# Two-layer encoder on one core: odd heads' maxima moved, attention outputs read back early, four norms computed by token halves

## The reference, cut to what matters

```python
for l in range(2):
    sh1, sc1, g1, sh2, sc2, g2 = split(silu(c) @ ada_w[l] + ada_b[l], 6)   # 48 columns of 128 ("mods")
    if l == 1: k, v = shared_kv(modulate(x, kv_g, kv_shift, kv_scale))
    h = modulate(x, norm1_g[l], sh1, sc1)          # rmsnorm(x) * g * (1 + sc) + sh
    y = fox_attention(h) if l == 0 else sliding_window_attention(h, k, v)   # both end in @ w_o
    x = x + g1 * y
    h = modulate(x, norm2_g[l], sh2, sc2)
    u = h @ w_up;  u = conv3(u);  x = x + g2 * ((silu(gate) * val) @ w_down)
return rmsnorm(x) * final_g
```

## Time and profile before

| | |
|---|---|
| median of three runs | 2446.96 us (2446.95 to 2448.36) |
| profiled execution | 2450.65 us, of which the span of instructions is 2448.8 us |
| busy in the span | PE 2309.4, PE weight loads 1922.2, DVE 1535.8, ACT 1147.6, POOL 1173.5 us |
| granted TensorE clock, mean | 0.973 of 2.4 GHz |

### The profile page before, as it was taken

The page is one execution under the profiler, slowest core; times in us unless marked ns, Lnnn a source line. Parts: engine busy times, 40 slices in busy tenths (PEclk is TensorE's granted clock), DMA queues, the critical chain, the costliest instruction groups (busy, mean ns, idle before and its releaser), DMA issues.

```text
span 2448.8 us, 30449 instructions
## 1 busy us (share of the span) xinstructions
PE 2309.4 (94%) x10984; PEld 1922.2 (78%) x10984; DVE 1535.8 (63%) x2470; ACT 1147.6 (47%) x1934; POOL 1173.5 (48%) x1580
## 2 busy tenths in 40 slices
PE   5999999998989999999999899989899999999996
PEld 3778788886767888888888688878678888888884
DVE  6575656657677677777665686882564444545546
ACT  4475665748145333333333476771443333333334
POOL 5411313120546766666666352214366666666650
PEclk8999999999999999999999999989999999999998
DMA  7111211112831333333331313133111111111111
GB/s 266 53 48 35 69 35 55 42 56 78 309 112 42 117 121 121 121 125 123 124 119 59 127 34 77 53 110 122 35 43 52 52 52 57 56 52 52 52 52 69
DMA packets 66007, 206.91 MB, mean 84 GB/s; under 512 B 7345, under 2 KB 7985, under 8 KB 65730
## 3 DMA queue, kind: packets, MB, share of 16 engines
q1 hardware_dynamic: 29760, 109.06, 14.0%
q10 hardware_dynamic: 36098, 95.91, 12.0%
HBM read 186.66 MB, written 16.32 MB: 83 GB/s over the span
## 4 chain that ended last, share of the span: by engine, by line
PE 80%; DVE 9%; ACT 6%; DMA 3%; issue 2%; SPq 0%; POOL 0%; ACTq 0%; DVEq 0%
PE bank L917 50%; PE bank L632 19%; PE bank L792 1%; PE bank L766 1%; DVE H L1658 1%; PE bank L827 1%; PE bank L802 1%; PE bank L1088 1%; PE bank L828 1%; PE bank L829 1%; ACT PF L1226 1%; DMA ada_raw<-in_ada_t 1%; PE bank L648 1%; DVE tn L1653 1%; DVE ada_raw L1669 1%
## 5 line engine op out<-in xcount | busy, mean ns | idle before, releaser
L917 PE MATMUL bank<-H,w_spl 128*128 128x512 f32 x3744 | 872.3, 392 | 19.3 <-DVE H L1658 14.6
L917 PEld LDWEIGHTS bank<-H,w_spl 128*128 128x128 f32 x3744 | 708.0, 189 | 171.7 <-issue 16.2
L561 POOL TENSOR_TENSOR w_spl<-w_raw,w_spl 128x256 fp32r<-128x256 f32 x688 | 536.7, 808 | 426.7 <-ACT w_spl L1380 425.2
L632 PE MATMUL bank<-H,w_spl 128*128 128x512 f32 x2016 | 509.9, 401 | 19.1 <-DVE H L1658 11.6
L917 PE MATMUL bank<-TB,w_spl 128*128 128x512 f32 x2112 | 492.6, 389 | 0.0
L917 PEld LDWEIGHTS bank<-TB,w_spl 128*128 128x128 f32 x2112 | 396.1, 188 | 83.3 <-issue 0.8
L632 PEld LDWEIGHTS bank<-H,w_spl 128*128 128x128 f32 x2016 | 378.4, 193 | 98.1 <-issue 12.6
L1380 ACT ACTIVATE w_spl<-w_raw 128x512 fp32r<-128x512 f32 x328 | 196.8, 624 | 356.3 <-PE bank L917 300.5
L499 POOL TENSOR_TENSOR pace<-one_s 128x1 f32<-128x1 f32 x50 | 13.1, 262 | 682.9 <-PE bank L792 350.5
L1934 DVE SCALAR_TENSOR_TENSOR X<-bank,mods,X 128x1024 f32<-128x1024 f32 x176 | 225.2, 1280 | 45.5 <-PE bank L917 44.7
L1927 DVE TENSOR_TENSOR bank<-bank,sU 128x512 f32<-128x512 f32 x80 | 55.9, 699 | 302.6 <-PE bank L917 302.6
(11 more groups left out here) (172 smaller groups left out, 3180.1 us busy)
## 6 DMA issues: line engine op xcount, KB each, us to landing
w_raw<-in_w_stream SPq DMA_DIRECT2D x184, 512.0 KB, 3.7
ada_raw_f<-in_ada_t ACTq DMA_DIRECT2D x128, 256.0 KB, 2.9
ada_raw_o<-in_ada_t ACTq DMA_DIRECT2D x8, 2048.0 KB, 7.7
ada_raw<-in_ada_t SPq DMA_DIRECT2D x8, 1024.0 KB, 18.9
negF<-scratch_f ACTq DMA_DIRECT2D x16, 512.0 KB, 3.7
X<-in_x_t SPq DMA_DIRECT2D x4, 1024.0 KB, 10.9
X<-in_x_t ACTq DMA_DIRECT2D x4, 1024.0 KB, 8.3
scratch_x<-X ACTq DMA_DIRECT2D x1, 4096.0 KB, 12.7
```

The lines of the kernel that those rows point to most:

```text
L561: last = pool.tensor_tensor(block_at(layer, b, 1, q, q + 256), src[:, q:q + 256], block_at(layer, b, 0, q, q + 256).bitcast(F32), ALU.subt ...
L632: last = pe.matmul(dst, stat(k, a), mov(k, b), start=(k == 0 and a + b == 0), stop=(k == KT - 1 and a == 1))
L917: last = pe.matmul(dst, block_at(layer, b, x, k * P, k * P + P), mov(y), start=(start and x + y == 0), stop=(stop and x == 1), skip_group_ ...
```

## The change

1. **Maxima.** All heads use one row of `MAX_T` (it was another for the second head of a group), negation at task 8. So that the next q/k pair is there, `FILL_1` is 3 steps at four tasks and 2 at ten (it was 2 at sixteen).
2. **Head pairs early.** Pairs 0 to 5 are loaded at tasks 13 and 14 of the last group into Hf[:, k, 1] (the place of H's low part; ACT first waits for the last q/k step) and split at tasks 16 to 26; pair 6 at 34 and 41. O_rawA is gone.
3. **Output projection's first tile** of layer 0, k = 0 to 6, is issued at tasks 25 to 44 of the last group; k = 7 comes inside tile 1 (`out_two`).
4. **Mods.** For tiles 4 to 7 the g2 product leaves the output projection (three instead of four) and goes as 8 half products to pairs 2 and 3 of the FFN; the other 128 shift by one pair.
5. **Norms by halves.** The last two output tiles run half by half (6 and 7 of tokens 0 to 511, then 6 and 7 of 512 to 1023); the square sum and rstd of the first half are made while the second is multiplied, and the next stage (`first_pair`, K) starts with all k of half 0. So does the last down projection (`last_down`: all 8 tiles of half 0, then of half 1). Squares of the FFN's end are added by POOL. `t_sums` and the first `taps` change places, and `high(0, s)` of pair 2 comes after two copies.
6. **Shared K/V.** X * rstd is written into X itself, after SP has stored that half of X to DRAM, so `modulate(3)` needs no product of its own. The bias is loaded by SP, behind the second store.
7. **The end**: one DVE operation X * gain * rstd per half tile into Y (eight tiles of its own), 16 output DMAs of 256 KB on SP.

```diff
-MAX_T = [[2, 1, 1, 1, 1, 1, 1, 2, 2, 0, 0, 0], [0, 0, 2, 1, 2, 1, 2, 1, 2, 1, 0, 0]]
-MAX_T.append(MAX_T[0])
+MAX_T = [2, 1, 1, 1, 1, 1, 1, 2, 2, 0, 0, 0]
-FILL_1 = [2] * 16
+FILL_1 = [3] * 4 + [2] * 10
+HEADS_LOADS = {13: (0, 1, 2), 14: (3, 4, 5), 34: (6,)}
+HEADS_SPLITS = {16: 0, 18: 1, 20: 2, 22: 3, 24: 4, 26: 5, 41: 6}
+OUT_A_BESIDE = {25: (0,), 28: (1,), 31: (2,), 34: (3,), 37: (4,), 40: (5,), 44: (6,)}
...
+            def square_sum(n, h):
+                at_end = n == 4 and h == 1
+                pe.wait_ge(ss_done, SS_0[n] + (6 * h + 6 - at_end if n in (2, 4) else 6 + h))
+                pe.matmul(bank(h), ones[:], ss[:, half_of(h)], start=True, stop=False)
...
+                pe.matmul(bank(h), ones[:], sq_at(n, 7, h), start=False, stop=True).then_inc(sum_ps, 1)
...
+                    if g == NG - 1:
+                        out_first(0, OUT_A_BESIDE.get(T, ()))
...
+            def out_last(layer):
+                for h in range(2):
+                    for m in (LAST, LAST + 1):
+                        if h == 0:
+                            pe.wait_ge(w_ready, tile_order([W_OUT_A, W_OUT_B][layer] + m) + 1)
+                            pe.wait_ge(wo_ev, 10 * layer + m - 1)
+                        for k in range(KT):
+                            last = product(bank(4 + 2 * ((m + 1) % 2) + h), w_tile([W_OUT_A, W_OUT_B][layer] + m),
...
+                            if h == 1 and m == LAST and k == SUM_OUT:
+                                square_sum(1 + 2 * layer, 0)
...
+                    for h in range(2):
+                        for k in range(KT):
...
+                            pe.wait_ge(h_lo, H_0[[1, 4][layer]] + 8 * h + k + 1)
...
+                            if h == 0 and k == SUM_NEXT[1 + 2 * layer]:
+                                square_sum(1 + 2 * layer, 1)
...
+            for m in range(8):          # act: the squares of the last down tiles
+                down_square(0, m, 0)
+            for m in range(4):
+                down_square(0, m, 1)
+            root(2, 0)
...
+            tile(W_KV)                  # gpsimd
+            for m in range(1, 7):
+                add_squares(2, m, 0)
+            for m in range(1, 4):
+                add_squares(2, m, 1)
+            tile(W_KV + 1)
+            for m in range(4, 7):
+                add_squares(2, m, 1)
...
+                for m in range(LAST):   # vector: out_proj
                     if layer == 0:
                         mods_of_tile(m)
+                        if m == LAST - 1:
+                            mods_of_tile(LAST)
...
+                residual(LAST, 0)
+                add_squares(n, LAST - 1)
+                add_squares(n, LAST, 0)
+                residual(LAST + 1, 0)
+                half_scaled(hn, 0, 0)
+                half_scaled(hn, 1, 0)
+                residual(LAST, 1)
...
                 for kk in range(4):
+                    if kk == 2:
+                        taps(0, 0, pair(0))
+                        taps(0, 1, pair(2))
                     t_sums(kk)
...
-            for k in range(8):
-                scaled(5, k, y_done)
+            for h in range(2):
+                dve.wait_ge(rs_done, 1 + 2 * 3 + h + 1)
+                for k in range(KT):
+                    V_.scalar_tensor_tensor(Y[:, k, half_of(h)], X[:, k, half_of(h)], gain[:, G_FIN + k:G_FIN + k + 1],
+                                            rstd[:, half_of(h)], ALU.mult, ALU.mult).then_inc(y_done, 1)
```

More of the change, by code:

```diff
@@ L1347, in _ @@
             load_ada(1)
-            for m in range(7):
-                squares(1)(m)
+            for m in range(LAST - 1):
+                out_square(0, m)
                 load_ada(m + 2)
+            load_ada(7)
+            out_square(0, LAST - 1)
             def ffn(layer):
-                n0, d0 = BLOCKS * layer, 88 * layer
+                n0, d0 = BLOCKS * layer, 96 * layer
                 def t_high(kk, which):
@@ L1950, in ffn @@
                 for kk in range(4):
+                    if kk == 2:
+                        taps(0, 0, pair(0))
+                        taps(0, 1, pair(2))
                     t_sums(kk)
-                for p in range(NORMAL):
-                    taps(p, 0, pair(4 * p))
-                    taps(p, 1, pair(4 * p + 2))
-                    gated(p)
+                gated(0)
+                taps(1, 0, pair(4))
+                taps(1, 1, pair(6))
+                gated(1)
                 for p in range(NORMAL, PAIRS):
-                    with_ada = layer == 0 and p in ADA_PAIRS
@@ L2018, in _ @@
                 last.then_inc(kb_lo, 1)
-            modulate(3)
+            for k in range(KT):
+                low(3, k)
             for b in range(4):
```

668 lines of the change are left out of this document (428 added, 240 removed).

## The result

The changed kernel takes 2423.14 us (median of four runs, 2421.15 to 2426.74) beside 2447.66 us of the kernel before on the same chip: 0.990 of it, 95% interval 0.9883 to 0.9917, so 1% faster. The forecast was 2384 us, range 2371 to 2404. The direction was right; of the 63 us that were summed up, 29.7 came between the two profiled executions, and 24.5 between the medians.

The account below looks back on a forecast made before the run. PE was busy 2309.4 of 2448.8 us, so only its idle holes and half-clock time could be won. Gains 5 + 0 + 9 + 11 + 25 + 13 = 63 us off 2450.65, median 3.7 lower: 2384 us, range 2371 to 2404.

Parts of the forecast that it names:

- attention: All head groups, with moved maxima, fill and splits: about 5 us gained, bounds 0 and 10.
- output norms: Norm by halves between output projection and FFN: gain 9 us in layer 0 (bounds 5, 13), 11 in layer 1 (8, 15).
- four land in head 13 ... so it does not shrink (24 us): Last attention group: four of six forward-moved splits fall in head 13, DVE load about 22 us, head stays at 24.
- 0.8 us a group: Attention: gain from spreading the maxima over tasks 0 to 8, 0.9 us in the first group.
- Tile 0 beside the group: Layer 0 output tile 0 beside the last heads: gain 0, bound 10 us, since tile 2 waits for loads.
- output tile 0 pays: Rival: PE, not the loads, sets tile 2's start, 10 us more gained, 2374 us; chance 0.07.
- a new stall of 6.3 us: First Strassen pair of layer 1's FFN: PE waits for ACT's first product copy, 52.7 to 59.0 us behind tile 7.
- Norm behind FFN 0, K/V, queries, bias: From FFN 0's last down projection to the sliding window's scores: 25 us gained, bounds 19 and 27.
- K's half 0 ends at 36.6: K of the shared K/V: its first half ends 36.6 us behind the start of the last down projection.
- End: From FFN 1's last down projection to the kernel's end: 37.5 us against 50.9, gain 13, bounds 10 and 15.
- The second: Rival: helpers on DVE, ACT and POOL bind the halves in four norms, costing up to 20 us, 2400; chance 0.27.
- rival 3: Slower: idle stretches keep PE at its low clock level for long, gains are eaten, 2450 us; chance 0.03.

Follow-up runs that it names:

- e5: Changed kernel with head pairs still loaded early, but pairs 0 to 5 split at tasks 25 to 35: 2419.03 us, 0.987 of the kernel before.
- e1: Changed kernel with head pairs loaded and split late, as in the kernel before, and output tile 0 whole behind attention: 2414.96 us, 0.9863 of the kernel before.
- e2: Changed kernel with loads behind attention reordered: X's first quarter, ada 0, second quarter, ada 1, rest of X: 2416.17 us, 0.9864 of the kernel before.
- e6: Changed kernel loading X's first quarter, then ada 0, behind attention, the rest of X and ada 1 once ada 0 landed: 2415.88 us, 0.9858.
- e10: Changed kernel with e5, e6 (row of c ahead of ada 0), e3 and ACT's high part as a plain copy together: 2401.90 us, 0.9809.
- e11: As e10, but with e1's late head pairs and tile 0 behind attention in place of e5: 2399.45 us, 0.9804 of the kernel before.
- e3: Changed kernel with two product copies and two high parts moved earlier in ACT's queue at both FFN starts: 2412.56 us, 0.985 of the kernel before.
- e14: Changed kernel with most GpSimd square additions and its splits of two K/V weight tiles cut to 4 columns: 2419.47 us, one run.
- e13: e11 without the plain copy, plus DVE's first sum, ACT's third copy and hidden tiles' parts first in layer 1: 2402.28 us, 0.9815.

## Why the prediction missed, step by step

**What bounds the kernel, and the holes.** Right: every hole named closed where the change closes it. What failed is the count of what comes behind it: the price of the early splits in head 13, and the chain of ACT and DVE in front of the first product copy (output norms) and of K's half 0. Three terms came out below their own lower bounds: attention (0 forecast at worst, -4.75 measured), and the output norms (5 and 8 at worst, 0.4 and 1.3).

**Attention: "four land in head 13 ... so it does not shrink (24 us)".** The place was right, the size was off by 6.1 us (30.1), and "over 27 us" for this head was among the prediction's own signs of being wrong. The splits' busy time was priced, about 1 us each, but not that this work delays exp on ACT, and with it PE, in a head that had just lost 12 matmuls of fill, and that PE's matmuls then take 3.6 us longer, at a granted clock of 0.83. e5 and e1 show 5.3 us for the splits and 2 for the loads. "0.8 us a group" for the maxima was 0.0 in the last group (e1), and the first three groups, forecast to win 2.5, ended 0.2 us later than before. The group took 104.0 us where the sum had 96.7. Together that is 10 of the 33 us that were missing.

**Tile 0 beside the group: 0.** Right, and for the reason given: tile 2 started 25.7 us behind attention, PE idle for 13.4, on the residual of tile 0 (e2 and e6 move it by moving the loads). The rival "output tile 0 pays" is refuted further than was asked: with the loads in the better order it pays nothing either (e10, e11).

**Output norms: 9 and 11, measured 0.4 and 1.3.** The forecast saw the new wait at ACT's copy, "a new stall of 6.3 us", beginning 52.7 us behind tile 7 and ending at 59.0. It began at 58.4 and ended at 65.9, with 2.4 us more in slow matmuls behind it; the product S4 (at 785.92) started at 71.6 instead of 63.4, and 73.3 before. So the mechanism was right, and the chain ahead of it was mis-sized: `first_pair` alone took 27.6 us where 22.7 were forecast, waiting for low parts and at a clock of 0.94. The FFN's halves on DVE: 16 of "1.28 us each, ACT twice 0.6" were 1.43 us each, as ACT's modulation of 512 columns takes 0.80 us; beside the weight split DVE's operations took 1.1 to 1.2 us instead of 0.69; and the first t_sums began 25.0 us behind tile 7 instead of 20. In the forecast's own count, from the end of tile 7, 11 us were to come and 3.2 and 3.4 came; another 1.7 and 2.1 went ahead of it, of which the sum had the 2 of layer 0 and nothing for layer 1. e3 shows that 4.5 and 7.0 us hang on nothing but the place of two copies, with the high parts beside them, in ACT's queue. What is left is close to DVE's own work, 50.1 us busy of the 55.4 behind tile 7.

**Norm behind FFN 0, K/V, queries, bias: 25, measured 20.5.** The queries, the scores, the bias (6.2 us of the 20.5, 5.6 forecast) came as forecast. "K's half 0 ends at 36.6" was wrong: 42.5. Half 0 was costed with DVE operations at their bare duration; e14 gives GpSimd's share of K, 3.0 us. The rest of it was not taken apart by a run; e14's rows show where it lies, in ACT's and DVE's own work for each k and in the chain behind the second sum.

**End: 13, measured 12.95,** by its own terms: 38.0 us behind the start of the last down projection, 37.5 forecast.

**The rivals.** The second, that halves are bound by their helpers, is what happened in both output norms and K, and its price, up to 20 us, was the size of what these terms fell short (22.8), though e3 shows that half of that was a place in a queue. It had a chance of 0.27. Its time, 2400, was still too low, as it left attention and the stall's size as they were; and its own price, 16 x 0.4 us in four norms, is 25.6 us and not 20. The range stood on the rivals' times. Added up, the terms' lower bounds give a gain of 42 us, or 2405; what was measured lies beyond that too. No run showed a slow stretch that feeds on itself (rival 3); e13 has 0.985 of the clock.

## What to carry to other kernels

When a hole in front of a stage is closed, the engines that prepare the stage have lost the same time: add up their busy time from there to the next product that needs them before counting the hole as won, and look up in which place of its queue each small copy stands. Work moved forward into a full stretch is priced by the engine that it queues on, not by its own duration. And a helper on GpSimd is not free while DVE is on the path, even if neither waits for the other.

## What the runs showed of the hardware

- DVE's subtraction or product of two SBUF operands, 512 columns: 0.68 to 0.69 us alone, 1.22 to 1.25 beside GpSimd's 256-column instructions, 0.69 beside its 4-column ones (e14).
- ACT, 512 columns from SBUF: 0.80 us with a scale and a bias for each partition, 0.63 as a plain copy.
- DVE's residual of 512 columns, with one big operand in PSUM and one in SBUF: 0.74 us beside GpSimd's 256-column additions and 0.75 beside the 4-column ones.
- A row of 4 KB written to all partitions counts with what it writes: in e6 some 3.6 MB moved before ada 0 had landed, where X's quarter and ada 0 are 3.1. With that row ahead of ada 0 (e10, e11) the time from the first issue to ada 0's landing was 13.5 and 12.7 us, with it behind (e6) 11.5. That the row's place is the reason was not tested alone.
